# Part of the first modulation moved from TensorE to VectorE and ScalarE in a trunk layer of a diffusion model

## The reference, cut to what matters

```python
mod = (jax.nn.silu(cond) @ P['w_ada'][l] + P['b_ada'][l]).reshape(cond.shape[0], N_MOD, D_MODEL)
shift1, scale1, gate1, shift2, scale2, gate2 = (mod[:, i, None, :] for i in range(N_MOD))
h = rmsnorm(x, P['g_pre_mix'][l]) * (1 + scale1) + shift1
(na_q, na_k, na_v, m_q, m_k, m_v, m_o, m_i, m_f, cv_b, cv_c, cv_x, gate_pre) = jnp.split(
    h @ P['w_in'][l], SPLIT_IDX, axis=-1)
...
```

## Time and profile before

| | us |
|---|---|
| median of 3 runs | 1154.02 |
| lowest, highest | 1150.59, 1154.95 |
| the profiled execution | 1151.45 |
| its span in the trace | 1149.7 |

### The profile page before, as it was taken

The page is one execution under the profiler, slowest core; times in us unless marked ns, Lnnn a source line. Parts: engine busy times, 40 slices in busy tenths (PEclk is TensorE's granted clock), DMA queues, the critical chain, the costliest instruction groups (busy, mean ns, idle before and its releaser), DMA issues.

```text
span 1149.7 us, 18622 instructions
## 1 busy us (share of the span) xinstructions
PE 1130.7 (98%) x7398; PEld 1062.9 (92%) x7398; DVE 719.3 (63%) x1282; ACT 471.4 (41%) x874; POOL 70.7 (6%) x122
## 2 busy tenths in 40 slices
PE   5999999999999999999999999999999999999997
PEld 4799999889999999999999988999999999988886
DVE  4524545448675566588795446899997777633444
ACT  4344443443334333322222337655555555533431
POOL 1032110000000000220000002100000000000002
PEclk9999999999999999999999999999999999999999
DMA  9566121132531121345654244234422232315112
GB/s 363 195 193 147 55 74 56 38 92 75 80 68 56 56 66 64 110 128 181 204 173 141 66 139 151 85 129 147 129 82 103 75 115 106 111 56 198 58 37 91
DMA packets 40006, 129.17 MB, mean 112 GB/s; under 512 B 8720, under 2 KB 10288, under 8 KB 38512
## 3 DMA queue, kind: packets, MB, share of 16 engines
q1 hardware_dynamic: 36592, 121.41, 32.7%
q0 software_dynamic: 3328, 6.57, 2.1%
HBM read 120.59 MB, written 7.36 MB: 111 GB/s over the span
## 4 chain that ended last, share of the span: by engine, by line
PE 96%; DVE 2%; ACT 1%; DMA 1%; issue 0%; SPq 0%; POOL 0%; POOLq 0%; ACTq 0%; DVEq 0%
PE ps L2014 29%; PE ps L2016 29%; PE ps L2015 29%; PE ps L2219 1%; PE ps L2258 1%; PE ps L2242 1%; PE ps L2310 1%; PE ps L2314 1%; PE ps L2312 1%; PE ps L2061 1%; DMA xt<-in_x_sample 1%; PE ps L2296 0%; PE ps L2186 0%; PE ps L2298 0%; PE ps L2243 0%
## 5 line engine op out<-in xcount | busy, mean ns | idle before, releaser
L2016 PE MATMUL ps<-h_hi,w_lo 128*128 128x320 f32 x1184 | 366.5, 310 | 0.0
L2014 PE MATMUL ps<-h_hi,w_hi 128*128 128x320 f32 x1024 | 323.3, 316 | 0.2 <-DVE w_hi L1567 0.2
L2015 PE MATMUL ps<-h_lo,w_hi 128*128 128x320 f32 x1024 | 317.0, 310 | 0.0
L2016 PEld LDWEIGHTS ps<-h_hi,w_lo 128*128 128x128 f32 x1184 | 222.9, 188 | 0.0
L1442 DVE TENSOR_TENSOR w_lo<-raw,w_hi 128x1024 fp32r<-128x1024 f32 x109 | 132.6, 1226 | 111.2 <-ACT w_hi L1084 110.7
L2014 PEld LDWEIGHTS ps<-h_hi,w_hi 128*128 128x128 f32 x1024 | 193.2, 189 | 2.4 <-DVE w_hi L1567 0.5
L2015 PEld LDWEIGHTS ps<-h_lo,w_hi 128*128 128x128 f32 x1024 | 193.1, 189 | 0.1
L2014 PE MATMUL ps<-w_hi,h_hi 128*128 128x512 f32 x380 | 150.8, 397 | 0.2 <-DVE h_lo L1717 0.2
L2016 PE MATMUL ps<-w_hi,h_lo 128*128 128x512 f32 x380 | 148.1, 390 | 0.0
L2015 PE MATMUL ps<-w_lo,h_hi 128*128 128x512 f32 x380 | 148.0, 389 | 0.0
L1084 ACT ACTIVATE w_hi<-raw 128x1024 fp32r<-128x1024 f32 x109 | 113.2, 1052 | 32.9 <-PE ps L2016 32.3
(11 more groups left out here) (268 smaller groups left out, 1826.4 us busy)
## 6 DMA issues: line engine op xcount, KB each, us to landing
raw<-in_w_blocks SPq DMA_DIRECT2D x182, 512.0 KB, 3.7
ada<-in_w_first SPq DMA_DIRECT2D x8, 1024.0 KB, 18.0
xline<-x SPq DMA_DIRECT2D x5, 512.0 KB, 5.0
x<-xline SPq DMA_DIRECT2D x5, 512.0 KB, 8.0
xt<-in_x_sample SPq DMA_DIRECT2D x4, 512.0 KB, 6.5
vtok<-vline POOLq DMA_DIRECT2D x8, 256.0 KB, 11.2
g<-gline SPq DMA_DIRECT2D x2, 1024.0 KB, 6.9
xb<-in_x_sample SPq DMA_DIRECT2D x4, 512.0 KB, 5.0
```

The costliest lines, as they stand in the source:

```text
L2014: nc.tensor.matmul(dst, wh, xh, start=first, stop=False, skip_group_check=resumed)
L2015: nc.tensor.matmul(dst, wh, xl, start=False, stop=False, skip_group_check=resumed)
L2016: return nc.tensor.matmul(dst, wl, xh, start=False, stop=last, skip_group_check=resumed)
```

## The change

Chunks 0 to 4 keep their two small products on PE. For chunks 5, 6 and 7 the pair (scale, shift) is computed on DVE: `w_first` holds those three blocks transposed on the host (one channel per partition), GpSimd loads `cond_rows` spread over all partitions into `condr0` (1 MB in SBUF) once the tokens' buffers have been read, ACT applies Silu to it ("dots_in"), and DVE does two multiply-and-sum instructions per chunk and half ("dot": 12 instructions for three chunks), followed by bias and norm weight. The dots are spread over the plan's steps k = 0 to 4 as 1, 2, 1, 1, 1. Scale and shift ("h") of chunks 3 to 7 move from DVE to ACT. The buffers are in space that the tokens' `xt` has left.

```diff
+DOT_CHUNKS = (5, 6, 7)
...
+    dots = [(k, m) for k in DOT_CHUNKS for m in range(2)]
     for k in range(KD):
+        c = k + 2
         plan.append(("first", k, 0, 2))
-        if k + 2 < KD:
-            rows(k + 2)
+        if c < DOT_CHUNKS[0]:
+            rows(c)
         plan.append(("first", k, 2, TT))
-        if k + 2 < KD:
-            columns(k + 2)
-            if k % 2 == 0:
-                split_to(k // 2 + 2)
-            plan += [("h", k + 2), ("hsplit", k + 2)]
+        if c < DOT_CHUNKS[0]:
+            columns(c)
+        if k % 2 == 0 and c < KD:
+            split_to(k // 2 + 2)
+        if k == 0:
+            plan.append(("dots_in",))
+        if c < KD:
+            plan += [("h", c), ("hsplit", c)]
+        for _ in range((1, 2, 1, 1, 1, 0, 0, 0)[k]):
+            plan.append(("dot", *dots.pop(0)))
...
+        condr0 = at("condr0", [P, 2, D], R1)
+        prod0s = [at(f"dot{c}", [P, D], R1 + 8192 + 4096 * c) for c in range(2)]
...
-                    sp.wait_ge(gemm_done, gid("ada_row", ("first", KD - 1)) + 1)
+                    sp.wait_ge(gemm_done, gid("ada_row", ("first", DOT_CHUNKS[0] - 1)) + 1)
...
+            pool.wait_ge(x_tr, 2 * TT)
+            src = bass.AP(a["cond_rows"].tensor, 0, [[0, P], [D, 2], [1, D]])
+            pool.dma_start(condr0[:, :, :], src).then_inc(condr0_in, 16)
             pool.wait_ge(const2_in, 16)
...
+                elif step[0] == "dots_in":
+                    act.wait_ge(condr0_in, 16)
+                    nc.scalar.activation(condr0[:, :, :], condr0[:, :, :], ACT.Silu).then_inc(condr0_rd, 1)
+                elif step[0] == "h" and step[1] > 2:
+                    k = step[1]
+                    act.wait_ge(xt_dve, TT)
+                    if k in DOT_CHUNKS:
+                        act.wait_ge(dot_bias, DOT_CHUNKS.index(k) + 1)
+                        act.wait_ge(dot_mod, DOT_CHUNKS.index(k) + 1)
+                    else:
+                        act.wait_ge(dve_drain, drains("V", gid("ada_pair", ("first", k))))
+                        act.wait_ge(mod_in, k + 1)
+                    for c, sl in ((0, slice(0, LAT)), (1, slice(LAT, T))):
+                        ins = nc.scalar.activation(xnt[:, k, sl], xnt[:, k, sl], ACT.Identity,
+                                                   scale=mod[:, 0, k, c:c + 1], bias=mod[:, 1, k, c:c + 1])
+                    ins.then_inc(h_aff, 1)
...
-                elif step[0] == "h":
+                elif step[0] == "dot":
+
+                    k, m = step[1:]
+                    dve.wait_ge(condr0_rd, 1)
+                    dve.wait_ge(ada_in[k], 16)
+                    n = 2 * DOT_CHUNKS.index(k) + m
+                    if n:
+                        dve.wait_ge(dot_done, n)
+                    for c in range(2):
+                        ins = nc.vector.scalar_tensor_tensor(prod0s[c][:, :], ada0[:, k, m * D:(m + 1) * D], 1.0,
+                                                             condr0[:, c, :], ALU.mult, ALU.mult,
+                                                             accum_out=mod[:, m, k, c:c + 1])
+                    ins.then_inc(dot_done, 1)
+                    if m == 1:
+                        dve.wait_ge(dot_done, n + 1)
+                        v = mod[:, 0:2, k, :]
+                        bc = cols[:, R_BADA:R_BADA + 16].rearrange("p (m k) -> p m k", m=2)[:, :, k:k + 1]
+                        nc.vector.tensor_tensor(v, v, bc.to_broadcast([P, 2, 2]), ALU.add).then_inc(dot_bias, 1)
+                        dve.wait_ge(dot_bias, DOT_CHUNKS.index(k) + 1)
+                        v = mod[:, 0, k, :]
+                        nc.vector.scalar_tensor_tensor(v, v, 1.0, cols[:, R_GPM + k:R_GPM + k + 1].to_broadcast([P, 2]),
+                                                       ALU.add, ALU.mult).then_inc(dot_mod, 1)
+                elif step[0] == "h" and step[1] <= 2:
...
+    for k in DOT_CHUNKS:
+        given["w_first"][k] = first[:, :, :, k].transpose(3, 2, 0, 1).reshape(P, 2 * D)
```

More of the change, by code:

```diff
@@ L673, in program @@
         ms_one, nat_zero, ml_sc = sems("ms_one nat_zero ml_sc")
+        condr0_in, condr0_rd, dot_done, dot_bias, dot_mod = sems(
+            "condr0_in condr0_rd dot_done dot_bias dot_mod")
         condr_in, condr_rd, ada_done, gcol_rd, gl_tr, gl_row, gl_out, g1_in, g2_in = sems(
@@ L991, in _ @@
                     pool.wait_ge(gemm_done, gid("mifs", 0, 0, 1) + 1)
-                    pool.wait_ge(gemm_done, gid("ada_row", ("first", KD - 1)) + 1)
+                    pool.wait_ge(gemm_done, gid("ada_row", ("first", DOT_CHUNKS[0] - 1)) + 1)
                     nc.gpsimd.memset(bm[:, :, :, 256:NKEY], 0.0).then_inc(bias_zero, 1)
@@ L2400 @@
     given["w_mif"][:, :, 0:16] = x["w_in"][0, :, C_MIF:C_MIF + 16].reshape(KD, P, 16).transpose(1, 0, 2)
-    given["w_first"] = np.ascontiguousarray(x["w_ada"][0, :, 0:2 * D].reshape(KD, P, 2, KD, P)[:, :, ::-1].transpose(
-        3, 1, 0, 2, 4).reshape(KD, P, KD * UW))
+    first = x["w_ada"][0, :, 0:2 * D].reshape(KD, P, 2, KD, P)[:, :, ::-1]
+    given["w_first"] = np.ascontiguousarray(first.transpose(3, 1, 0, 2, 4).reshape(KD, P, KD * UW))
+    for k in DOT_CHUNKS:
+        given["w_first"][k] = first[:, :, :, k].transpose(3, 2, 0, 1).reshape(P, 2 * D)
     b_ada = x["b_ada"].reshape(6, D)
```

## The result

| | before | after |
|---|---|---|
| median of 21 runs, us | 1153.72 | 1155.26 |
| lowest, highest | 1150.59, 1154.95 | 1154.69, 1156.83 |
| profiled execution, its span | 1151.45, 1149.7 | 1155.79, 1154.0 |

The ratio is 1.0020, with a 95% interval of 1.0014 to 1.0027: the changed kernel is 1.6 to 3.1 us slower. That is inside the half per cent called "no change" in the prediction. The forecast was +3.0 us; the ratio gives +2.3, the two medians +1.5. The spread changed more than the median: the times of the kernel before span 4.4 us, those of the changed one 2.1.

A forecast was written before the change was run, and what follows sets the result against it. PE, busy for 98% of the span, was taken as the bound; its 5.0 us saved would be spent waiting for DVE's chain, and 3.0 more. The median of 1154.02 plus 3.0 gave 1157.0 us, range 1152.0 to 1161.5.

The forecast's parts named there:

- PE's saving, 4.4 to 5.0 us: Three rows and three pairs leave PE's path in the first stage, each worth 1.47 to 1.67 us.
- Chunk 5's block at 33.9: On SP's queue, GpSimd's load pushes the landing of chunk 5's block back by 2.5 us, from 31.34 to 33.9.
- The condition rows near 25: GpSimd's 1.05 MB load, issued at some 18.7, takes 5.0 us at half the bandwidth and lands near 25 us.
- land late: Rival, chance 0.06: condition rows land after 27.8 and hold ACT; served only behind SP's queue, +8.6 us, 1162.6.
- S: Time from which DVE's chain of dots runs: 33.9 by chunk 5's block; with late condition rows, chunk 2's low part done.
- Chunk 3 ready at 39.5, PE idle for 1.9 us: After DVE's dot, drain and ACT's work, chunk 3 is ready at S + 5.6; PE wanted it at 37.57.
- Chunk 4 ready at 48.0, PE idle for 5.1 us: Two dots and a bias ahead of its pair's drain make chunk 4 ready at S + 14.1; PE ends chunk 3 at 42.9.
- ACT's scale and shift at 0.95: ACT's two instructions per chunk, moved from DVE, take 0.95 us, between bounds of 0.74 and 1.0 from other copies.
- mif at 59.6: Gate product on PE behind the chunks starts at S + 25.7 = 59.6 instead of 56.55, +3.0 us.
- the rival with 0.19: Slow clock after PE's gap, chance 0.19: chunk 4 takes 6.9 instead of 3.44 us, total +5.2; two slow chunks +8.6.
- 1157.0 us: Forecast time of the whole kernel: +3.0 us put on the median of 1154.02.
- +0.5 and +5.2: Ends of the range before widening: the load not pushed back (rival, 0.20) and one slow-clock chunk.

The follow-up runs named there:

- the reordered kernel: Changed kernel with the same 12 dots in another place of DVE's row, most behind the drains of chunks 3 and 4: 1151.23 us, ratio 0.9986 to the kernel before.
- the filled kernel: Changed kernel with four additional matmuls on PE ahead of chunk 1's pair, filling its wait for that chunk's row: 1155.11 us, ratio 1.0023 to the kernel before.
- both kernels filled: Kernel before and changed kernel, each with four additional matmuls in PE's wait for chunk 1's row: 1151.77 us (ratio 0.9996) and 1155.11 us (1.0023).

## Why the prediction was right, and where its steps were off

- **PE's saving, 4.4 to 5.0 us.** Measured 4.6 (3.2 to 6.1) with nothing in its place. The price was right.
- **Chunk 5's block at 33.9.** It landed at 9.27 + 24.4 = 33.7, and the first dot started at 33.78 with the load named as what it waited for. Right; without the rows' load the block landed 3.0 us earlier, at 30.7.
- **The condition rows near 25.** Wrong: they landed at 19.48 + 9.4 = 28.9. The load had taken 5.0 us next to one block; next to a full queue its 1.05 MB in 9.4 us are 112 GB/s, a quarter of the 421 that were moved, not half. The rule of "DMA: Bandwidth & Descriptors" in the Trainium skill held in that the load wasn't served last: it landed at 28.9, not near the 36 of a load behind SP's queue. It gives no share. So the condition of the rival "land late" came true, a landing behind 27.8: ACT waited 0.72 us for the rows, the Silu ran from 28.93 on and not between 26 and 29, which the prediction had named as a sign of being wrong. Yet it cost nothing on the path. By the prediction's own sum S is the landing plus 3.5, 32.4 here, and chunk 5's block came later, at 33.7; the rows would have had to land behind 30.2 to matter. In the reordered kernel, where PE was on time, the Silu held chunk 2's high part to 30.22, 0.4 us behind its scale and shift.
- **Chunk 3 ready at 39.5, PE idle for 1.9 us.** Ready at 39.30 (38.55 + 0.75). But PE wasn't idle: it was 1.9 us late itself (29.27 instead of 27.34 for chunk 1): 0.6 us from its start (chunk 0 at 22.81 instead of 22.25), and 1.4 from the clock's fall during chunk 0. In the filled kernel, where PE was on time, it did wait: 1.08 us for chunk 4's row on ACT, which the prediction had not placed there.
- **Chunk 4 ready at 48.0, PE idle for 5.1 us.** 47.6 and 4.55 us. Right; the reordered kernel shows that this order is the cause.
- **ACT's scale and shift at 0.95.** 1.20 us, above both bounds (0.74 and 1.0); the scaled 128x512 from SBUF wasn't in the rows. Three of them lie on the chain, 0.75 us too little. The dots made up for it by luck: two take 2.30 us until the next instruction, not 2.48, and there are six pairs.
- **mif at 59.6.** DVE and ACT had all ready at 59.2. It started at 60.72, since chunk 4 ran at half clock. That was the rival with 0.19 (+2.2 us on top), and the measured part is 1.1 to 1.5; the clock came back before the end of chunk 4, which took 6.0 us instead of the rival's 6.9. The prediction set the granted clock of 1.00 in the first stretch against the rule that it cites from the Trainium skill; that was the wrong row to weigh. In the executions profiled here the clock fell behind each of PE's waits of 2.65 us and more in this stage (five of them), and not behind the one of 1.35. The rule of "TensorE: Matmul & The Clock Gate" in the Trainium skill, section "HAM oscillation — how this bites in real kernels", held for the 4.55 us wait.
- **1157.0 us.** The forecast for the profiled execution was 1154.5 and it took 1155.8, one slow-clock cost more. Put on the median it was 1157.0 against 1155.26, too high by 1.7. The step that was off is the last one: +3.0 was added to a median that holds executions in which the clock fell during chunk 0. The changed kernel doesn't pay for that, because its chain starts at a load. For the undisturbed executions the shift is larger than the medians show: lowest against lowest it is 4.1 us, highest against highest 1.9. With both kernels filled it is 3.1 to 3.3. That this lies next to +3.0 is partly luck. In the profiles of the two filled kernels mif starts 2.9 us later (59.80 against 56.89). The slow clock, left out of the sum, puts in 1.3 (ACT was done at 58.46), and against it stand 0.8 from a block that landed at 33.0 instead of 33.9, 0.3 from the chain and 0.3 from the start of mif in the kernel before.
- **The range.** The text adds 2 us on either side of +0.5 and +5.2, which gives 1152.5 to 1161.2; it says 1152.0 to 1161.5. The measured time lies in both.

So the mechanism was right: dots ahead of the drains, DVE waiting for chunk 5's block, and a long wait of PE ahead of chunk 4. What the prediction had wrong is what the clock does behind waits, on both sides of the comparison.

## What to carry to other kernels

Work moved to an engine with idle time still costs what stands behind it in that engine's row: put it where the engine waits anyway (here between a drain and the low part, while ACT works), never ahead of a small drain that others wait for. How much to move is less clear: against the kernel before, eight dots behind the drains gain about 2.5 us, twelve there 1.6, and twelve in the wrong place lose 2.3. Eight against twelve is not shown, since their intervals overlap (0.9967 to 0.9987 and 0.9977 to 0.9994). Before adding a shift to a median, look at whether the new critical chain still passes through what spreads the runs.

## What the runs showed of the hardware

- TensorE's granted clock fell to half behind waits of 2.65 to 4.6 us (five of five), and behind the 1.8 us wait ahead of chunk 0 in five of nine profiled executions; matmuls of 128x512 then came every 0.43 us instead of 0.23. In the changed kernel that lasted for about 12 matmuls (47.75 to 53.0). Matmuls without use in the wait kept it at 1.00.
- The 1 MB load on GpSimd's queue took 9.3 to 10.6 us beside a full SP queue (seven profiles), 5.0 beside one block.
- While GpSimd wrote 128x2048 in SBUF, DVE's scale and shift of 128x512 and 128x128 took 1.64 us instead of 0.80 (one profile; no run shows whether the one is the cause of the other).
- Two ACT instructions with scale and bias from SBUF, 128x512 and 128x128, take 1.20 us, against 0.80 on DVE and 0.74 for a plain ACT copy of 128x640.
